# A two-block transformer kernel with its bias rows, its attention order and its query rows rearranged

## What is computed

```python
h = rmsnorm(x, norm_mix_pre[l])
qa, ka, va, pu, qc, kc, vc, gl = split(h @ w_in[l])
ya = softmax(rope(rmsnorm(qa)) @ rope(rmsnorm(ka)).T) @ va     # "A": 8 heads of 64, 512 x 512 scores
yb = pool_mixer(pu, w_pool[l], pool_scale[l])                  # windows of 2, 4, 8, 16 tokens
yc = neighbourhood_attention(qc, kc, vc, rpb[l])               # "C": 8 heads, windows of 8 x 16 in a grid of 8 x 64,
                                                               #      scores + bias rpb[head, row distance, column distance]
merged = sum(sigmoid(gl + b_gate[l]) * ([ya, yb, yc] @ w_branch[l]))
x = x + rmsnorm(merged @ w_out[l], norm_mix_post[l]);  x = x + rmsnorm(conv_gated_mlp(...), ...)
# second block, "D": three dilated causal branches (128 keys at strides 1, 4, 16) of 8 heads of 128, mixed by their denominators
q = rms_norm(x, mix_pre_g[1]) @ w_q;   k, v = rms_norm(x, kv_norm_g) @ w_kv
```

## Time and profile before

| | us |
|---|---|
| median of 3 runs | 3315.86 |
| lowest, highest | 3313.65, 3316.20 |
| the profiled execution, its own time | 3318.09 |
| its span, first to last instruction | 3316.3 |
| mean granted clock of TensorE in it | 0.986 of 2.4 GHz |

### The profile page before, as it was taken

How to read it: one execution, slowest core, us unless ns; L and a number is a source line. 1 busy time by engine, 2 the same in 40 slices (tenths; PEclk the granted TensorE clock), 3 DMA queues, 4 the chain that set the end, 5 groups by cost and what they waited for, 6 DMA issues and landing times.

```text
span 3316.3 us, 42241 instructions
## 1 busy us (share of the span) xinstructions
PE 3167.2 (96%) x17113; PEld 2608.9 (79%) x17113; DVE 1688.1 (51%) x2228; ACT 1198.9 (36%) x1612; POOL 159.4 (5%) x171
## 2 busy tenths in 40 slices
PE   5989999999989899999999889999899999999999
PEld 5766888888877588888887568888788888788887
DVE  3465455553444744565527855552543534555543
ACT  2444224342333622444323254442322212344432
POOL 3030000000021200000002110000000000000000
PEclk8999999999999999999999999999999999999999
DMA  6121323322342032332322123223221121222222
GB/s 144 58 68 52 96 94 102 101 90 93 100 86 74 26 102 89 102 101 94 101 96 78 52 67 104 89 95 102 84 89 64 64 89 62 70 92 96 94 89 89
DMA packets 230545, 285.03 MB, mean 86 GB/s; under 512 B 5156, under 2 KB 188492, under 8 KB 230412
## 3 DMA queue, kind: packets, MB, share of 16 engines
q1 hardware_dynamic: 225628, 266.89, 24.9%
q0 software_dynamic: 4784, 16.24, 2.3%
HBM read 281.02 MB, written 2.10 MB: 85 GB/s over the span
## 4 chain that ended last, share of the span: by engine, by line
PE 83%; DVE 10%; ACT 3%; issue 2%; DMA 1%; POOL 0%; DVEq 0%; SPq 0%; ACTq 0%; POOLq 0%
PE ps L1566 18%; PE ps L1567 18%; PE ps L1568 18%; PE ps L1679 6%; PE ps L1681 6%; PE ps L1680 6%; DVE t_wlo L1022 2%; ACT t_whi L664 2%; DMA t_wraw<-in_w_in_dram 1%; PE ps L1605 1%; PE ps L1604 1%; PE ps L1603 1%; DVE t_vb L1486 1%; PE ps L2098 1%; DVE t_x L1067 1%
## 5 line engine op out<-in xcount | busy, mean ns | idle before, releaser
L1022 DVE TENSOR_TENSOR t_wlo<-t_wraw,t_whi 128x2048 fp32r<-128x2048 f32 x252 | 579.7, 2300 | 1324.8 <-ACT t_whi L664 1324.8
L1566 PE MATMUL ps<-t_hh,t_whi 128*128 128x512 f32 (+1 forms) x2704 | 1012.9, 375 | 14.6 <-DVE t_accv L1216 5.1
L1567 PE MATMUL ps<-t_hl,t_whi 128*128 128x512 f32 (+1 forms) x2704 | 1003.8, 371 | 0.0
L1568 PE MATMUL ps<-t_hh,t_wlo 128*128 128x512 f32 (+1 forms) x2704 | 1003.7, 371 | 0.0
L664 ACT ACTIVATE t_whi<-t_wraw 128x2048 fp32r<-128x2048 f32 x252 | 482.6, 1916 | 1385.8 <-PE ps L1568 962.3
L1566 PEld LDWEIGHTS ps<-t_hh,t_whi 128*128 128x128 f32 x2704 | 511.8, 189 | 116.7 <-issue 17.0
L1567 PEld LDWEIGHTS ps<-t_hl,t_whi 128*128 128x128 f32 x2704 | 512.0, 189 | 88.0 <-issue 2.4
L1568 PEld LDWEIGHTS ps<-t_hh,t_wlo 128*128 128x128 f32 x2704 | 511.7, 189 | 87.3
L1679 PE MATMUL ps<-t_whi,t_midh 128*128 128x512 f32 x704 | 274.4, 390 | 0.0
L1681 PE MATMUL ps<-t_whi,t_midl 128*128 128x512 f32 x704 | 274.0, 389 | 0.0
L1680 PE MATMUL ps<-t_wlo,t_midh 128*128 128x512 f32 x704 | 273.9, 389 | 0.0
(11 more groups left out here) (277 smaller groups left out, 3728.8 us busy)
## 6 DMA issues: line engine op xcount, KB each, us to landing
t_wraw<-in_w_in_dram SPq DMA_DIRECT2D x46, 1024.0 KB, 5.3
t_wraw<-in_w_up_dram SPq DMA_DIRECT2D x44, 1024.0 KB, 5.1
t_wraw<-in_ffn_w_in_dram SPq DMA_DIRECT2D x44, 1024.0 KB, 5.1
t_wraw<-in_w_kv_dram SPq DMA_DIRECT2D x24, 1024.0 KB, 5.2
t_wraw<-in_w_down_dram SPq DMA_DIRECT2D x20, 1024.0 KB, 5.1
t_wraw<-in_ffn_w_out_dram SPq DMA_DIRECT2D x20, 1024.0 KB, 5.0
t_wraw<-in_w_branch_dram SPq DMA_DIRECT2D x12, 1024.0 KB, 5.0
t_wraw<-in_w_q_dram SPq DMA_DIRECT2D x12, 1024.0 KB, 5.1
```

The lines of the kernel that those rows point to most:

```text
L1022: v.tensor_tensor(wlo[slot][:, :], wraw[slot][:, :], whi[slot][:, :].bitcast(F32), ALU.subtract).then_inc(w_lo, 1)
L1566: te.matmul(out, wh, xh, start=first, stop=False)
L1567: te.matmul(out, wh, xl, start=False, stop=False)
L1568: return te.matmul(out, wl, xh, start=False, stop=last)
```

## The change

- **Bias rows.** The 8 copies take 16 contiguous runs of 114 x 31 floats instead of 16 x 113 runs of 32, and GpSimd makes `t_e` from them with 32 instructions of 128 columns per layer instead of 16 of 256. In layer 0 it now waits for the low parts of the first rows before it issues them.
- **Pair loops of C and A.** Scores stand two pairs ahead and behind the first turn of the iteration: TensorE makes scores(1) before the loop, then turn 2j, scores(j+2), weigh(j-1), turn 2j+1. VectorE goes divide 2j+1, maxima of j+2, divide 2j+2, and A's factor is applied once per pair. `t_pC` has four slots; the maxima of C's head n wait until head n-4 is turned. The chunk parts in C move from pair 3 to 7.
- **Around A.** scores(0) stand in the middle of pu's second chunk; its copy and the low part of the next chunk go into the loop (pairs 0 and 16). Half of the first gate chunk's products stand behind A's last turn, the other half behind the last weighing. The merge's first round is written out.
- **D.** The chunks of the first head pair go k, v, k, v, k, q, q, q, v; the query rows are split and turned in gaps behind chunks 0 and 1; copies out of PSUM are made of two banks apart.

The core of the diff; hunks left out are the same edits in places that the text names.

```diff
+        D_ORDER = [[(kD, 0), (vD, 0), (kD, 1), (vD, 1), (kD, 2), (qD, 0), (qD, 1), (qD, 2), (vD, 2)]]
+        D_ORDER += 3 * [[(kD, 0), (vD, 0), (qD, 0), (kD, 1), (vD, 1), (qD, 1), (kD, 2), (qD, 2), (vD, 2)]]
...
+                if l == 0:
+                    pool.wait_ge(h_lo, SPLIT["pre0"] + 8)
                 for r in range(ROWS_C):
-                    src = bass.AP(tensor=A["rpbp"].tensor, ap=[[1, 16], [31, 113], [1, 32]],
+                    src = bass.AP(tensor=A["rpbp"].tensor, ap=[[1, 16], [1, 114 * 31]],
...
+                    pool.dma_start(rpb_rows[16 * r:16 * r + 16, 0:114 * 31], src).then_inc(rpb_in, 16)
...
-                        at = (2 * hp + s) * 15 * 32
-                        raw = rpb_rows[:, at:at + WIN].rearrange("p (r k) -> p r k", k=32)
-                        halves = raw.rearrange("p r (h k) -> p h r k", h=2)
-                        middle = raw[:, :, 8:24].rearrange("p r (o k) -> p o r k", o=1).broadcast_to([P, 2, ROWS_C, 16])
-                        for i, rows in enumerate((halves, middle)):
-                            at = (2 * s + i) * WIN
-                            ins = gp.tensor_tensor(
-                                e2[hp][:, at:at + WIN].rearrange("p (h r k) -> p h r k", h=2, k=16),
-                                cmask[:, i * WIN:(i + 1) * WIN].rearrange("p (h r k) -> p h r k", h=2, k=16), rows, ALU.subtract)
+                        for i in range(2):
+                            for h in range(2):
+
+                                at = (2 * hp + s) * 15 * 31 + (8 if i else 16 * h)
+                                rows = rpb_rows[:, at:at + ROWS_C * 31].rearrange("p (r k) -> p r k", k=31)[:, :, 0:16]
+                                to = (2 * i + h) * P
+                                ins = gp.tensor_tensor(
+                                    e2[hp][:, 2 * s * WIN + to:2 * s * WIN + to + P].rearrange("p (r k) -> p r k", k=16),
+                                    cmask[:, to:to + P].rearrange("p (r k) -> p r k", k=16), rows, ALU.subtract)
                     ins.then_inc(e2_ready, 1)
```

ScalarE's program, pair loop and pu:

```diff
-                if pre == "pre6":
-                    for b in range(4):
-                        row_hi("hq", qh, b, 2 + b % 2)
...
+                slots = 4 if kind == "C" else SLOTS
+
                 def exp(n):
                     g = n0 + n
-                    s, q = g % SLOTS, g % 4
+                    s, q = g % slots, g % 4
...
-                    if n >= SLOTS:
-                        act.wait_ge(turned, g - SLOTS + 1)
+                    if kind == "A" and n >= slots:
+                        act.wait_ge(turned, g - slots + 1)
...
-                pair_attention("C", STEPS[f"C{l}"], pC, {3: lambda c=c: hi(c + 5)})
+                pair_attention("C", STEPS[f"C{l}"], pC, {7: lambda c=c: hi(c + 5)})
...
-                for j in range(2):
-                    hi(c + j)
...
+                def pu_rows(j, b, W=W):
...
+                def second_pu(c=c):
+
+                    act.wait_ge(w_used, c + 2)
+                    pu_rows(1, 4)
+
+                hi(c)
+                pu_rows(0, 2)
+                act.wait_ge(head_sum, 5 * l + 5)
+                sc.activation(rq[:, 0:32], bank(5)[:, 0:32], ACT.Sqrt, bias=epsc).then_inc(head_std, 1)
...
+                between = {j: lambda g=g: pooled_hi(g) for g, j in enumerate(POOL_PAIRS)}
+                between[0] = second_pu
+                between[16] = lambda c=c: hi(c + 1)
+                pair_attention("A", STEPS[f"A{l}"], pA, between)
...
+                    if hp == 0 and j < 2:
+                        row_hi("hq", qh, 2 * j, 2)
+                        row_hi("hq", qh, 2 * j + 1, 3)
```

VectorE's program, maxima and loop, then D:

```diff
-                if pre == "pre6":
-                    scale_row("hq", 0)
-                    scale_row("hq", 1)
-                    for b in range(4):
-                        row_lo("hq", qh, ql, b, 2 + b % 2)
-                        if b < 2:
-                            scale_row("hq", b + 2)
...
+            def pair_maxima(n0, j, scores_in, factors):
+
+                q = (n0 + 2 * j) % 4
+                for n in (2 * j, 2 * j + 1):
+                    dve.wait_ge(scored, n0 + n + 1)
+                    ins = scores_in(n, (n0 + n) % 4, q + n % 2)
+                    if not factors:
+                        ins.then_inc(maxed, 1)
+                if factors:
+                    ch.link(ins)
+                    v.tensor_tensor(small[:, q:q + 2], small[:, 4 + q:6 + q], factors(2 * j), ALU.mult).then_inc(maxed, 2)
...
-            def pair_attention(n0, pbuf, scores_in, scale, pair_out, extra, per=4):
+            def pair_attention(n0, pbuf, scores_in, factors, pair_out, extra, per=4):
                 pairs = 4 * per
-                negated_max(n0, 0, scores_in, scale)
-                negated_max(n0, 1, scores_in, scale)
+                pair_maxima(n0, 0, scores_in, factors)
                 divide(n0, pbuf, T)
                 for j in range(pairs + 2):
                     if j < pairs:
                         divide(n0 + 2 * j + 1, pbuf, T)
-                    if j == 0 and j in extra:
-                        extra[j]()
+                    if j == 0:
+                        if j in extra:
+                            extra[j]()
+                        pair_maxima(n0, 1, scores_in, factors)
+                    if j < pairs - 2:
+                        pair_maxima(n0, j + 2, scores_in, factors)
                     if j < pairs - 1:
-                        negated_max(n0, 2 * j + 2, scores_in, scale)
-                        negated_max(n0, 2 * j + 3, scores_in, scale)
                         divide(n0 + 2 * j + 2, pbuf, T)
...
-                    if n >= SLOTS:
-                        dve.wait_ge(turned, STEPS[f"C{l}"] + n - SLOTS + 1)
+                    if n >= 4:
+                        dve.wait_ge(turned, STEPS[f"C{l}"] + n - 3)
...
-                lo(c + 1)
-                dve.wait_ge(pu_in, 2 * l + 2)
-                v.memset(small[:, 16:17], 0.0).then_inc(drained, 1)
+
+                def second_lo(l=l, c=c):
+                    lo(c + 1)
+                    dve.wait_ge(pu_in, 2 * l + 2)
+                    v.memset(small[:, 16:17], 0.0).then_inc(drained, 1)
...
+                if hp == 0:
+                    scale_row("hq", 0)
+                    scale_row("hq", 1)
+                for i in range(8):
+                    qkv_out(i)
+                    if hp == 0 and i < 2:
+                        row_lo("hq", qh, ql, 2 * i, 2)
+                        row_lo("hq", qh, ql, 2 * i + 1, 3)
+                        if i == 0:
+                            scale_row("hq", 2)
+                            scale_row("hq", 3)
+                c += 9
```

TensorE's program, pair loop, A's start, first gate, D:

```diff
             def pair_attention(kind, n0, scores, pbuf, weigh, v_drained=None, behind=None, extra={}):
                 pairs = 8 if kind == "C" else 16
+                scores(1)
                 for j in range(pairs + 1):
-                    if j < pairs - 1:
-                        if j:
-                            pe.wait_ge(probs if kind == "A" else maxed, n0 + 2 * j)
-                        scores(j + 1)
                     if j < pairs:
                         turn_probs(n0, 2 * j, pbuf)
+                    if j < pairs - 2:
+                        pe.wait_ge(probs if kind == "A" else maxed, n0 + 2 * j + 2)
+                        scores(j + 2)
                     if j in extra:
                         extra[j]()
...
+                    if j == 0:
+                        pe.wait_ge(pu_in, 2 * l + 2)
...
-                start(c + 1, d=d + 1)
-                rows_out(c + 1, (hh, hl), bank0=0).then_inc(w_used, 1)
-                pe.wait_ge(head_std, 2 * l + 2)
-                pe.wait_ge(qk_ready, 6 * l + 6)
-                pe.wait_ge(drained, 2 + d + 2)
...
+                pe.wait_ge(w_lo, c + 2)
+                pe.wait_ge(qk_ready, 6 * l + 4)
+                row_tile(c + 1, (hh, hl), 0, bank(4))
+                pe.wait_ge(head_std, 2 * l + 2)
+                pe.wait_ge(qk_ready, 6 * l + 6)
                 scores_a(0)
+                row_tile(c + 1, (hh, hl), 1, bank(5)).then_inc(w_used, 1)
...
+                def first_gate(c=c, d=d):
+                    start(c, d=d)
+                    row_tile(c, (hh, hl), 0, bank(6))
+
                 pair_attention("A", STEPS[f"A{l}"], scores_a, pA, weigh_a(l),
+                               behind=first_gate,
                                extra={j: lambda g=g: pooled_out(g) for g, j in enumerate(POOL_PAIRS)})
+                row_tile(c, (hh, hl), 1, bank(7)).then_inc(w_used, 1)
                 pe.wait_ge(y_lo, PAIRS[f"A{l}"] + 4)
-
                 pe.wait_ge(pool_lo, 4 * l + 4)
-                c, d = FIRST[f"merge{l}"], DRAINS[f"merge{l}"]
-                with pe.Fori(0, 3) as n:
+                gate_rows(0, 0, 1)
+                branch_rows(0, 0)
+                for j in range(2):
+                    gate_rows(0, 1, j)
+                branch_rows(0, 1)
```

(16 more changed lines are left out.)

145 lines of the change are left out of this document (72 added, 73 removed).

## The result

| | before | after |
|---|---|---|
| median, us | 3316.2 (5 runs, 3313.65 to 3320.1) | 3298.6 (5 runs, 3291.9 to 3301.9) |
| profiled execution, its span | 3318.09, 3316.3 | 3301.90, 3300.1 |
| mean granted clock | 0.986 | 0.989 |

The ratio is 0.9944, 95% interval 0.9931 to 0.9957: 18 us faster where 47 were forecast. The start and D came out as forecast; layer 1's bias rows brought nothing, and the pair loops of C and A cost most of what the rest had brought.

The account below looks back on a forecast made before the run. TensorE, busy 96% of the span, was taken as the bound, so gains lie in its idle or half-clock time. Terms -19.8, +1, -7.9, +2.5, -14.5, -8.8, +0.4 sum to -47.1; 3318.09 - 47.1 - 2.2 = 3268.8 us, range 3248 to 3290.

Parts of the forecast that it names:

- Start: Layer 0's start: with bias rows issued later, the first product starts at 13.35 rather than 33.12, -19.8 us.
- Layer 1's bias rows: Layer 1's C chunks: the slow weight chunk beside the bias rows goes, -7.9 us (-7 to -8.5).
- C's ring: C's pair loop: dependency cycle through transposes, scores, weighing, maxima and divide, 4.93 us per pair, +2.5 us over both layers.
- rival 2: C's loop: TensorE, 66% busy, falls to half clock in three of six pairs a layer, +19, 3288 us; chance 14%.
- the row at 1900: Trace evidence held against a falling clock: from 1900 to 1905 the upper level held with 3.11 of 5 us busy.
- A: end: End of attention A: half the first gate chunk behind the last transpose covers waits, -2.5 us a layer.
- start: Start of attention A: scores 0 inside pu's second chunk bring pair 1's first transpose to 221.0, -7.25 us a layer.
- loop: Attention A's pair loop: 3.97 us per pair against 3.71 before, +2.5 us a layer after the last pairs.
- D: Start of D: TensorE's wait and half-clock products go, -8.8 us (-6 to -9); smaller PSUM copies cost +0.4.
- the spill of the bias products: Layer 0's start: GpSimd's 32 half-size subtractions hold up VectorE's reads, +1 us (0 to 2).
- rival 3: Loops of C and A: the clock stays at 1.2 GHz throughout, together +105, 3374 us, slower than before; chance 3%.
- The rival in which the order brings what it can: Loops of C and A: slot waits and VectorE's order cost nothing, 3.26 us per pair, 3231 us; chance 8%.

Follow-up runs that it names:

- e1: The kernel before with only the bias-row part of the change: 3300.4 us, ratio 0.9945.
- e4: The changed kernel with one wait added, so layer 1's bias products come in two groups around a low part: 3286.9 us, ratio 0.9903.
- e2: The changed kernel with the pair loops' order of before, scores one pair ahead: 3282.8 us, ratio 0.9893.
- e6: The changed kernel with needless work, each pair of C weighed a second time behind its second transpose: 3295.6 us, ratio 0.9939.
- e3: The changed kernel with VectorE dividing head 2j+2 ahead of the maxima of pair j+2: 3253.2 us, ratio 0.9803.
- e13: A repeat of the changed kernel that weighs C's pairs twice, run beside the changed kernel: 3293.7 us.
- e8: The changed kernel with divide before maxima and grouped bias products, but bias rows in 128-byte runs with 16 wide subtractions: 3252.6 us, ratio 0.9808.

## Why the prediction went wrong, step by step

- **Start: right** (-19.8 forecast, -20.4). The high part of chunk 0 moved from 33.14 to 13.60, as row 1's high part ends at 13.70. I called that "the first product"; the first product came at 22.32, from 42.42. The difference holds, the place was misnamed.
- **Layer 1's bias rows: the step failed.** The prediction says: "The two differ by the slow chunk of the earlier trace rows and by nothing else I find, so that goes". It did go, and gave nothing (0.0 for -7.9), since VectorE's low part now waited for GpSimd's products, 7.68 instead of 2.29, and TensorE's clock fell on top. e1 shows the same with this part alone, e4 the 8.0 once they are apart. I had priced this contention at 0 to 2 us, in layer 0 only, where it cost nothing here and 0.8 to 1.1 in e2 to e4, and had put it at nothing in layer 1, although before both stood side by side there too (2.80 instead of 2.29). The Trainium skill, "SBUF — State Buffer", section "Who interferes with whom", has a VectorE instruction with two inputs in SBUF contend with a GpSimd instruction that reads SBUF, for ports that only one of them holds at a time. The traces agree: 2.77 for one of GpSimd's 0.73, or 7.68 for VectorE's 2.29. The same section says that the order of issue decides who is blocked. That isn't what after shows, as far as the recorded starts tell: the low part, begun at 918.88, let 13 instructions of GpSimd pass that began behind it.
- **C's ring: right in kind, 4.93 forecast and 5.07 measured at full clock; wrong in size in the sum** (+2.5 for both layers, +17.6). This was rival 2, the clock that falls in a ring with TensorE two thirds busy, and its sign, a granted clock under 1.00 for more than a pair, is there. It priced three of six pairs at 3.2 each, +19 in all over the forecast, and the profile shows +15. That this is so near is partly luck: nearly every pair of after's loop is long, but by 1.6 (6.63 - 5.07), since each runs at half clock only in part. I gave it 14% because of the row at 1900. That row is of a stage of many small products, with waits of 1.16 and 0.99 in other places, and it was no neighbour of this ring. The Trainium skill's rule ("TensorE: Matmul & The Clock Gate", section "A second HAM failure mode: psum-queue depth-cycling"), set aside there, is of short idle stretches between groups of products with which the clock swings between both levels. C's window above agrees in kind: 0.74, with no wait over 1.74 in the loop, though the wait here is for a divide of VectorE, and one loop of six stayed at 1.00.
- **A: end right, start 1.2 short, loop priced too low.** In after's own frame the first transpose of pair 1 came 6.05 earlier (7.25 forecast), the end gave 2.5 a layer, as forecast, and the ring is 3.95 at full clock (3.97). The start is short of its forecast because the factor of the first pairs takes 0.67 and 0.97 in place of my 0.1, and the loop cost 7.0 and 4.6, not 2.5, since divides take up to 1.31 in place of 0.49 while GpSimd makes the pool windows beside them, and in layer 0 the clock falls on top (0.83 from 205 to 225). At 221.04, when GpSimd's row has ended, the factor is back at 0.16 and the divide at 0.49; no run moves these windows, so that GpSimd is the cause is argued from the times and not tested. VectorE's rows of both instructions, and GpSimd's beside them, from after's timeline:

```profile
208.17 0.97 DVE L1174 TENSOR_TENSOR t_small<-t_small,t_rq 128x2 f32<-128x2 f32 x1
...
215.18 1.29 DVE L1155 TENSOR_SCALAR t_pA<-t_pA,t_small 128x512 f32<-128x512 f32 x1
```

```profile
206.93 2.20 POOL L604 TENSOR_TENSOR t_win<-t_win 128x525 f32<-128x525 f32 x2
...
213.99 3.61 POOL L604 TENSOR_TENSOR t_win<-t_win 128x525 f32<-128x525 f32 x3
```

  A in total: -14.5 forecast, -5.4 measured.
- **D: right** (-8.8 and +0.4 forecast; -11.1, and +0.5 behind it). The 2.3 beyond the forecast are no part of its reasoning: before, TensorE's clock was at half level for 6.8 us at 2357, ahead of D, and in after it isn't. e6 has the same D and still has that stretch, at 2339, and gives 9.0. TensorE is busy for the whole of the window in after, at full clock:

```profile
2376.00:2400.00 24.00, 24.00 (x153) 1.00 0.36 113
```

- **Sum.** -47.1 forecast, -16.2 in the profiled execution: +7.9 layer 1, +15.1 C, +9.1 A, +2.7 conformer stage, -0.6 start, -1.0 the spill of the bias products that did not come, -2.3 D. One sum of the prediction has a slip that changes nothing: in rival 3, 6.5 less 3.97 is 2.5 a pair and not 2.4, so +71 and not +67. The range ended at 3290 because I took rival 2 as the worst that could befall the loops, and as an alternative to the forecast rather than as a thing that adds to a second miss.
- **The chances.** Faster was right. The rival in which the order brings what it can (3231) fell, and e3 shows what it lacked: one exchange on VectorE.

## What to carry to other kernels

Moving a producer earlier helps only if every engine's own order lets its consumer go first: write down the new ring with each engine's program order in it, and ask which instruction stands behind one that depends on the ring's other end. Count a ring's idle share as a risk to TensorE's clock, priced at the half-clock durations of all its steps, and added to the forecast, not set beside it. Where two engines' instructions fall side by side and one is reshaped or moved, count the case in which the other waits for the whole row, here 3.9 to 7.5 us, and not only for one instruction.

## What was not expected of the hardware

- Idle stretches of 1.74 us in a ring of 5.07 (16.29 of 24 us busy at full clock) let the clock fall to 0.74 on average over 26 us. The same ring held 1.00 in one layer of one profile, and, with 21.55 of 25 us busy (e6, layer 0), in all four C loops of e6 and e13.
- One 128 x 2048 subtraction of VectorE, 2.29 us alone, beside GpSimd's row of 32 short ones either gets through in 2.32 to 2.64, and one of GpSimd's waits, or waits until the row is over, 6.22 to 9.84 in all, while GpSimd loses nothing (12.8 for the row).
- While the bias rows fly, windows of 4 us show 113 or 114 GB/s with runs of 14 KB (after, layer 1), 83 to 95 with runs of 128 bytes (before, layer 1) and 106 to 118 with these in e8, where 1 MB chunks move at 348 to 388: most of the loss is not the length of the runs. What it is no run shows.
